# Second norm's factors read from sums that every partition holds; the router's products in two column groups

## The reference

```
x = x + gt1 * (merged @ w_out)
u = rmsnorm(x, norm_ffn_w) * (1 + sc2) + sh2     # factor of a token: 1 / sqrt(mean(x*x) + 1e-6)
s = sigmoid(u @ router_w)                        # 64 experts
```

## Time and profile before

| | |
|---|---|
| runs | 2899.44 us median of 3 (2897.51 to 2901.99) |
| profiled execution | 2898.27 us, span 2896.5 us |
| PE busy, share of span | 2755.3 us, 95% |
| PEld | 1626.5 us, 56% |
| DVE | 1058.4 us, 37% |
| ACT | 572.8 us, 20% |
| POOL | 813.1 us, 28% |
| granted clock of PE, mean over the span | 0.971 |

### The profile page before, as it was taken

One profiled execution on the slowest core, in us unless ns is written; L12 is line 12 of the kernel. 1 busy time (PEld: TensorE's weight loads), 2 busy tenths in 40 slices (PEclk: granted clock), 3 DMA queues, 4 the chain that ended last, 5 costly groups with the idle time before them and its releaser, 6 DMA issues. The chain is left out here.

```text
span 2896.5 us, 31387 instructions
## 1 busy us (share of the span) xinstructions
PE 2755.3 (95%) x10366; PEld 1626.5 (56%) x10367; DVE 1058.4 (37%) x1635; ACT 572.8 (20%) x1074; POOL 813.1 (28%) x992
## 2 busy tenths in 40 slices
PE   7997999997999899999999898999999999999996
PEld 4564888864666556666666566444444444444443
DVE  3333233334657677832111273322222222222224
ACT  3213333324434200011000230111111111111112
POOL 1000222101334000000000012555655555565553
PEclk8998999998999999999999898999999999999997
DMA  6520000021010111212112120688777788888874
GB/s 239 226 96 25 16 16 23 15 67 33 23 44 23 46 28 34 72 33 80 48 26 102 46 104 0 233 283 270 242 250 208 257 300 280 282 265 264 294 241 145
DMA packets 162802, 382.19 MB, mean 132 GB/s; under 512 B 24595, under 2 KB 111711, under 8 KB 134793
## 3 DMA queue, kind: packets, MB, share of 16 engines
q1 hardware_dynamic: 130449, 311.52, 30.2%
q0 software_dynamic: 32256, 69.33, 10.4%
HBM read 339.65 MB, written 72.94 MB: 142 GB/s over the span
## 5 line engine op out<-in xcount | busy, mean ns | idle before, releaser
L2568 PE MATMUL ps<-big 128*128 x1536 | 675.5, 593 | 3.2 <-SPq L2495 1.8
L2568 PEld LDWEIGHTS ps<-big 128*128 128x128 f32 x1536 | 284.3, 190 | 325.7 <-issue 325.7
L2520 POOL DMA_INDIRECT big<-u_rows,big x384 | 393.7, 1025 | 169.9 <-issue 85.4
L1756 PE MATMUL ps<-big 128*128 128x352 f32 x1152 | 346.8, 461 | 5.7 <-SPq L1692 5.7
L2578 PE MATMUL ps<-big 128*128 x768 | 345.8, 593 | 3.4 <-ACT big L2632 3.4
L1756 PEld LDWEIGHTS ps<-big 128*128 128x128 f32 x1152 | 219.7, 191 | 129.1 <-SPq L1692 6.1
L2673 DVE SCALAR_TENSOR_TENSOR big<-big,ps 128x256 f32<-128x256 f32 x96 | 64.0, 667 | 570.9 <-ACT big L2622 570.7
L2578 PEld LDWEIGHTS ps<-big 128*128 128x128 f32 x768 | 145.4, 190 | 188.4 <-issue 188.4
L846 PE MATMUL ps<-big 128*128 128x352 f32 x576 | 206.0, 464 | 2.1 <-DMA big<-in_w_in 2.0
L1301 PE MATMUL ps<-big 128*128 128x352 f32 x576 | 187.1, 473 | 12.8 <-DVE big L1521 7.8
L2536 POOL DMA_INDIRECT y_rows<-big x96 | 155.9, 1624 | 126.6 <-issue 61.2
(11 more groups left out here) (557 smaller groups left out, 3120.7 us busy)
## 6 DMA issues: line engine op xcount, KB each, us to landing
big<-in_exp_w_gate SPq DMA_DIRECT2D x64, 1024.0 KB
big<-in_exp_w_up SPq DMA_DIRECT2D x64, 1024.0 KB
big<-in_exp_w_down SPq DMA_DIRECT2D x64, 1024.0 KB
big<-in_ada_w SPq DMA_DIRECT2D x24, 1024.0 KB, 7.5
big<-in_w_in SPq DMA_DIRECT2D x48, 512.0 KB, 4.1
big<-in_w_in SPq DMA_DIRECT2D x6, 1024.0 KB, 5.3
big<-in_w_branch SPq DMA_DIRECT2D x24, 256.0 KB, 4.5
big<-u_rows,big POOLq DMA_INDIRECT x384, 5.9
```

What stands on the lines that cost most here:

```text
L1756: ins = pe.matmul(ps[:, c, 0:CW], ring_g[:, q % 2, j, :], k.hT[:, j, c * CW:(c + 1) * CW], start=(j == 0), stop=(j == KT - 1))
L2520: g.indirect_dma_start(out=x_rows[:, u, x * 256:(x + 1) * 256], out_offset=None, in_=u_quarters, in_offset=bass.IndirectOffsetOnAxis(idx_i ...
L2568: ins = pe.matmul(ps[:, 2 + u, :].rearrange("p (g f) -> p g f", f=FF), xT[:, u, j, :], gate_up[:, j], start=(j == 0), stop=(j == KT - 1))
```

## The change

The root and the inverse are taken on all 128 partitions, from the sums as they stand there: ACT takes the root of 128 x 704 and 128 x 352 numbers, DVE inverts them in place in SBUF (`root`), and the multiplications read `root` where they read PSUM. The turn, the spread and their two semaphores go. One small Sqrt (`warm`, 128 x 1) is put at the start of ACT's program, ahead of the squares.

The router's 1056 tokens are cut into four quarters of `LW` = 264. Quarters 0 and 2 go to output partitions 0 to 63 as before, quarters 1 and 3 to partitions 64 to 127, in banks 3 and 4. So there are 32 products of 264 columns where there were 24 of 352. ACT copies two quarters of the logits out and DVE the other two.

```
-    rw, rstd, eps = w.take(KT, E_N), w.take(NT), w.take(1)
+    rw, eps, warm = w.take(KT, E_N), w.take(1), w.take(1)
+    LW = T // 4
...
-            pe.wait_ge(rooted, 2)
-            for t in range(NT):
-                n = tokens_of(t)
-                ins = pe.matmul(ps[0:n, 6, t:t + 1], root[0:1, t * P:t * P + n], k.ones[0:1, 0:1], start=True, stop=True)
-            ins.then_inc(turned, 1)
-            pe.wait_ge(inverted, 2)
-            for t in range(NT):
-                n = tokens_of(t)
-                out = ps[:, 1 + t // 4, (t % 4) * P:(t % 4 + 1) * P] if t < 8 else ps[:, 7, 0:NS]
-                ins = pe.matmul(out, bcast(rstd[0:n, t:t + 1], P), k.ident[0:n, 0:n], start=True, stop=True)
-            ins.then_inc(spread, 1)
...
             for j in range(KT):
                 pe.wait_ge(modulated, j + 1)
-                for c in range(NCH):
-                    ins = pe.matmul(ps[0:E_N, 3 + c, 0:CW], rw[:, j, :], k.hT[:, j, c * CW:(c + 1) * CW], start=(j == 0), stop=(j == KT - 1))
+                for q in range(4):
+                    ins = pe.matmul(ps[E_N * (q % 2):E_N * (q % 2) + E_N, 3 + q // 2, 0:LW], rw[:, j, :], k.hT[:, j, q * LW:(q + 1) * LW],
+                                    start=(j == 0), stop=(j == KT - 1))
...
+            act.wait_ge(eps_ready, 1)
+            act.activation(warm[:, :], eps[:, :], ACT.Sqrt)
             for m in range(KT):
...
-            act.activation(root[0:1, 2 * CW:T], ps[0:1, 0, 0:CW], ACT.Sqrt, scale=1.0 / D, bias=eps[0:1, :]).then_inc(rooted, 1)
+            act.activation(root[:, 2 * CW:T], ps[:, 0, 0:CW], ACT.Sqrt, scale=1.0 / D, bias=eps[:, :]).then_inc(rooted, 1)
...
-            act.activation(chunks(k.logits_T), ps[0:E_N, 3:6, 0:CW], ACT.Copy).then_inc(stopped, 1)
+            for q in (0, 2):
+                act.activation(k.logits_T[:, q * LW:(q + 1) * LW], ps[0:E_N, 3 + q // 2, 0:LW], ACT.Copy).then_inc(stopped, 1)
...
-            v.wait_ge(turned, 1)
-            v.reciprocal(rstd[:, 0:8], ps[:, 6, 0:8]).then_inc(inverted, 1)
-            v.reciprocal(rstd[0:NS, 8:9], ps[0:NS, 6, 8:9]).then_inc(inverted, 1)
-            v.wait_ge(spread, 1)
+            for r, cols in enumerate((slice(0, 2 * CW), slice(2 * CW, T))):
+                v.wait_ge(rooted, r + 1)
+                v.reciprocal(root[:, cols], root[:, cols]).then_inc(inverted, 1)
+            v.wait_ge(inverted, 2)
...
-                v.tensor_tensor(k.hT[:, j, 0:SEQ], k.xT[:, j, 0:SEQ], wide, ALU.mult).then_inc(normed, 1)
+                v.tensor_tensor(k.hT[:, j, 0:SEQ], k.xT[:, j, 0:SEQ], root[:, 0:SEQ], ALU.mult).then_inc(normed, 1)
...
+            v.wait_ge(logits, 1)
+            for q in (1, 3):
+                v.tensor_copy(k.logits_T[:, q * LW:(q + 1) * LW], ps[E_N:2 * E_N, 3 + q // 2, 0:LW]).then_inc(copied, 1)
```

More of the change, by code:

```diff
@@ L1958, in project_out @@
     sq, acc, root = w.take(2, T), w.take(T), w.take(T)
-    rw, rstd, eps = w.take(KT, E_N), w.take(NT), w.take(1)
+    rw, eps, warm = w.take(KT, E_N), w.take(1), w.take(1)
+    LW = T // 4
     filled, drained, added = k.sem("po_filled"), k.sem("po_drained"), k.sem("po_samples_added")
     router_loaded, shared_loaded, eps_ready = k.sem("po_router_loaded"), k.sem("po_shared_loaded"), k.sem("po_eps_ready")
-    squared, gathered, summed, rooted, turned, inverted, spread, normed, sampled, modulated, logits, dstep, stopped = (
-        k.sem("po_" + x) for x in ("squared", "squares_added", "summed", "rooted", "turned", "inverted", "spread", "normed", "sampled",
-                                   "modulated", "logits", "dve_step", "logits_copied"))
+    squared, gathered, summed, rooted, inverted, normed, sampled, modulated, logits, dstep, stopped, copied = (
+        k.sem("po_" + x) for x in ("squared", "squares_added", "summed", "rooted", "inverted", "normed", "sampled",
+                                   "modulated", "logits", "dve_step", "logits_copied", "logits_copied_by_vector"))
     zeroed, zeros_stored = k.sem("po_zeroed"), k.sem("po_zeros_stored")
@@ L2040, in _ @@
                 act.activation(sq[:, m % 2, :] if m else acc[:, :], k.xT[:, m, :], ACT.Square).then_inc(squared, 1)
-            act.wait_ge(eps_ready, 1)
             act.wait_ge(summed, 1)
-            act.activation(root[0:1, 0:2 * CW].rearrange("p (c w) -> p c w", c=2), ps[0:1, 6:8, 0:CW], ACT.Sqrt, scale=1.0 / D, bias=eps[0:1, :])\
+            act.activation(root[:, 0:2 * CW].rearrange("p (c w) -> p c w", c=2), ps[:, 6:8, 0:CW], ACT.Sqrt, scale=1.0 / D, bias=eps[:, :])\
                .then_inc(rooted, 1)
-            act.activation(root[0:1, 2 * CW:T], ps[0:1, 0, 0:CW], ACT.Sqrt, scale=1.0 / D, bias=eps[0:1, :]).then_inc(rooted, 1)
+            act.activation(root[:, 2 * CW:T], ps[:, 0, 0:CW], ACT.Sqrt, scale=1.0 / D, bias=eps[:, :]).then_inc(rooted, 1)
             for j in range(KT):
@@ L2066, in _ @@
                     v.tensor_tensor(acc[:, :], acc[:, :], sq[:, (m - 1) % 2, :], ALU.add).then_inc(gathered, 1)
-            v.wait_ge(turned, 1)
-            v.reciprocal(rstd[:, 0:8], ps[:, 6, 0:8]).then_inc(inverted, 1)
-            v.reciprocal(rstd[0:NS, 8:9], ps[0:NS, 6, 8:9]).then_inc(inverted, 1)
-            v.wait_ge(spread, 1)
+            for r, cols in enumerate((slice(0, 2 * CW), slice(2 * CW, T))):
+                v.wait_ge(rooted, r + 1)
+                v.reciprocal(root[:, cols], root[:, cols]).then_inc(inverted, 1)
+            v.wait_ge(inverted, 2)
             v.wait_ge(added, KT)
-            wide = ps[:, 1:3, :].rearrange("p a b -> p (a b)")
             scale = k.mod[:, 4 * KT:5 * KT, 1:NSEQ]
@@ L2075, in _ @@
             for j in range(KT):
-                v.tensor_tensor(k.hT[:, j, 0:SEQ], k.xT[:, j, 0:SEQ], wide, ALU.mult).then_inc(normed, 1)
+                v.tensor_tensor(k.hT[:, j, 0:SEQ], k.xT[:, j, 0:SEQ], root[:, 0:SEQ], ALU.mult).then_inc(normed, 1)
                 if j == 0:
-                    st(v.tensor_tensor(k.hT[:, :, SEQ:T], k.xT[:, :, SEQ:T], bcast(ps[:, 7, 0:NS].unsqueeze(1), KT, NS), ALU.mult))
+                    st(v.tensor_tensor(k.hT[:, :, SEQ:T], k.xT[:, :, SEQ:T], bcast(root[:, SEQ:T].unsqueeze(1), KT, NS), ALU.mult))
                     st(v.tensor_tensor(s, s, bcast(scale.unsqueeze(3), KT, SB, SL), ALU.mult))
                     v.tensor_tensor(s, s, bcast(k.mod[:, 3 * KT:4 * KT, 1:NSEQ].unsqueeze(3), KT, SB, SL), ALU.add).then_inc(sampled, 1)
+            v.wait_ge(logits, 1)
+            for q in (1, 3):
+                v.tensor_copy(k.logits_T[:, q * LW:(q + 1) * LW], ps[E_N:2 * E_N, 3 + q // 2, 0:LW]).then_inc(copied, 1)
 def plan_moe(k):
```

## The result

The changed kernel takes 2883.65 us in the median (2880.91 to 2891.41, 4 runs); the kernel before took 2899.26 beside it (2897.51 to 2901.99, 4 runs). A second series gave 2884.72 and 0.9944 [0.993, 0.9958], 16.2 us. Gains in us are worked out from such ratios unless the text says medians; here the medians lie 15.6 and 15.2 apart.

A forecast was written before the change was run, and what follows sets the result against it. The prediction took a chain of steps, one engine at a time, between sums and barrier to bound the block. Gains of 3.27 + 6.89 + 0.26 = 10.4 us gave 2889.0 us, with an 8-in-10 range of 2885.5 to 2894.0.

The forecast's parts named there:

- The factors: From sums to first multiplication: roots and inverses on all partitions replace turn and spread, gaining 3.27 us.
- The router: PE's router products: two column groups run side by side, so the router ends sooner, gaining 6.89 us.
- S: Time of the first multiplication by the factors, from which the router was counted: 1651.57 before, 1648.3 forecast.
- that case: Router with a clock that rises at once: ACT's tiles become the bound, bringing only 0.2 us more.
- The open loads: Rival in the router: weight loads no longer hide behind the shorter products; 6.3 us gained, 2893.2 us; chance 0.05.
- groups that do not overlap: Rival in the router: it keeps its 17.3 us, leaving 3.3 + 0.26 us gained, 2895.9 us; chance 0.06.
- The copies: Logits' copy after the router: ACT and DVE take two quarters each, gaining 0.26 us.
- the one from the block to the whole: At the barrier after the block: all later blocks start from it, so the 10.4 us saved come off the whole.
- a later wait takes it back: Rival in the routing block: 26 more low-clock products cost 5.7 us; 4.7 gained, 2894.7 us; chance 0.07.

The follow-up runs named there:

- bwarm: Kernel before plus idle products nobody reads on PE, ahead of the sums and in three placement waits: 2890.42 us, ratio 0.9965.
- awarm: Changed kernel plus idle products nobody reads on PE, ahead of the sums and in three placement waits: 2881.89 us, ratio 0.9935.
- bplace: Kernel before plus idle products in PE's placement waits only, none ahead of the sums: 2892.48 us, ratio 0.9977.
- roots: Kernel before with only the roots and inverses on all partitions and the early root; router and copy as before: 2887.68 us, ratio 0.9953.
- a2: Changed kernel unaltered, timed and profiled a second time: median 2884.72 us; its profiled execution took 2891.16 us.
- nowarm: Changed kernel without the early small Sqrt: 2882.98 us.
- bdelay: Kernel before plus two idle ACT copies of 900 columns ahead of the barrier: 2896.24 us, ratio 0.9986.
- lnexp: Changed kernel with idle products, factors as exp(-0.5 ln(mean)) on ACT instead of root and DVE inverse: 2877.22 us, ratio 0.9926.
- b2: Kernel before unaltered, profiled a second time: 2899.98 us.

## Why the prediction was right about the block and wrong about the whole

**The factors.** Forecast 7.9 us from the sums to the first multiplication, measured 7.72; the two inverses 6.76, forecast 6.90. The gain is 3.46 for 3.27. This held, and for the reason given, save that the early root was not needed for it.

**The router.** PE starts at S + 2.74 (forecast 2.72), the second tile at S + 4.94 (5.0), and the last product is through at S + 12.86 (13.14), S being 1646.61. The clock rose earlier than taken: it is 0.96 in the mean from 1653, S + 6.4, to 1660, where S + 8.5 stood in the sum. From there ACT's tiles are the bound, as the prediction had it for that case. 7.17 us gained for 6.89.

**The open loads and groups that do not overlap** are refuted by the step of 0.44 us a pair at the low clock. The Trainium skill states in "TensorE: Matmul & The Clock Gate", section "Part 3: Packing small matmuls", that weight loads overlap products in flight only where their row groups differ, which would put these loads in the open; the trace of the changed kernel disagrees, with 0.24 us of two loads hidden in each step of 0.44.

**The copies.** 0.79 on DVE, forecast 0.78.

So the work of the block ends at 1660.31, 21.42 us behind the sums, for 21.9 forecast and 32.29 before: 10.87 us gained for 10.4. One reading ahead of the sum was wrong and did no harm: of the second stretch in the earlier trace rows the prediction says that only one engine at a time has much to do, but PE, DVE and ACT are busy 7.24, 8.37 and 6.04 of its 10 us. It is the list of instructions that shows PE as the last of them, and the sum rests on that list.

**The step that failed** is the one from the block to the whole: "what is saved between the sums and the barrier should come off the whole, unless a later wait takes it back". It takes the routing block as a fixed length that only shifts, with one way out, a loss: 26 more of its products at the low clock. The price was seen (some 46 of the 144 products at the low clock in the earlier trace rows), but the start of the block was allowed to add low products and not to take them away. There were fewer of them: two of the three traces after have 36.9 us for the 144, where both before have 42.2, and the routing blocks are 1.7 to 7.1 us shorter than before. The bound below should have been the 32.0 us that the prediction itself gives for all products at the high clock: some 10 us more gain, so 2879 as the range's lower end; the time lies between. (Held at the high clock, in bwarm, awarm and bplace, they took 33.9 us, which makes it 8.3 us and 2880.7.)

That the routing block has no fixed length is shown: one program, roots, took 157.96 and 151.69 us. That this, and no error in the steps, is the surplus has three runs for it: with the clock held up in both kernels the difference of the medians falls to 8.5 us, with the spread given above; in the kernel before, holding it up in the placement alone gives 6.7 us; and a delay alone, which shortens no step, gives 4, with an interval that begins at 0.9.

**What stays open.** The timed executions leave no trace, so that most of the changed kernel's have the short routing block is inferred from their times (the eight without a trace took 2881 to 2886, the first two with one 2891), not seen; and a time does not tell the form, since a2 had the short one and took 2891.16. That the earlier start is what shortens the block is argued as well: two long ones of two before against two short ones of three after, with a further short one (152.81) in nowarm, can be chance between executions. Which start of the block leads to which form isn't settled either: 1674.63 gave the long one, 1675.67 in bdelay the short one, 1662.26 in the changed kernel the long one, and one program (roots) gave both. Behind the first of the three waits the products took 6.82 us where they began at 1746.23, in the kernel before, and 3.80 where they began at 1746.44, in bdelay. And the experts' block varied as well, with code that is the same in all: 1020.2 us in the first trace before, 1027.2 after, 1029.7 in a2, 1018.0 in lnexp. A part of that is PE's waits for the experts' weights, which SP's queue brings (the waits view from 1800 us on: total us, count, longest), before and after:

```profile
PE ps L2568 <- SPq L2495: 1.8, 1, 1.8
```

```profile
PE ps L2563 <- SPq L2490: 9.4, 3, 6.4
```

It hid half of the gain in the first pair of traces (2898.27 to 2891.41). In b2 the same wait sums to 5.0 us with the same code as 1.8, so I take it for spread between executions and not for a price of the earlier start; no run was made to tell these apart.

## What to carry to other kernels

A saving ahead of a barrier shifts all that follows, and a later stretch in which PE works in pieces between waits may have no fixed length, as the routing block here: look for products of one shape with two durations, and price both ends, all at the high clock and all that could be at the low one. To learn what a change itself is worth, hold that stretch fixed in both kernels, as idle products in PE's waits did here, and compare again. And when a long chain has been cut, the next link shows its price at once: two inverses over all partitions took 6.76 us, a logarithm and an exponential with a table load under four.

## What the runs showed of the hardware that was not expected

- More work, less time: 1.78 us of idle copies ahead of a barrier made the kernel 4 us faster (0.9986 [0.9975, 0.9997]). In its trace the 144 products take 35.6 us where they took 42.2, more of them at the high clock; that the delay brought this about is argued.
- Equal waits of PE, 3.26 us, left 16 equal products at 3.80, 5.19, 6.62 or 6.82 us.
- Two column groups of 64 with their weight loads ran in the time of one, 0.44 us a pair for 264 columns of f32 at the low clock.
- Once a single wait stood before the root, its table load was over 4.36 us before that wait ended; with two waits it came behind them.
